# Feed-forward block products by one level of Strassen's scheme in an encoder layer on one core

## The chip, the cores and the metric

The kernel runs on one core of a Trainium2 chip. The metric is the device time of one execution in microseconds (us), lower is better. A core has five engines with instruction streams of their own, which meet only at semaphores: TensorE (PE in the profile), VectorE (DVE), ScalarE (ACT), GpSimd (POOL) and SyncE (SP), which here only issues DMAs. SBUF is the core's working memory of 128 partitions, PSUM holds TensorE's sums in eight banks of 128 x 512 float32.

## The reference

A layer of a streaming encoder over 2048 tokens (and 16 leading meta tokens) of width 1024: an input projection, two attention branches, a gated mix, a residual with layer norm, then a gated feed-forward of inner width 2816 with another residual and layer norm. All in float32. The change is in the last two lines:

```python
mix = (g_a * y_a + g_b * y_b) @ w_out
h = layer_norm(DEEPNORM_ALPHA * h + mix, ln1_g, ln1_b)
ff = (jax.nn.silu(h @ w_ff_gate) * (h @ w_ff_up)) @ w_ff_down
return layer_norm(DEEPNORM_ALPHA * h + ff, ln2_g, ln2_b)
```

## The kernel before

The program has three parts, one after the other: projection and key selection, attention (from 1129 us of the span), and `mix_and_ffn` (from 2080 us), which holds all of the mix and the feed-forward. Each part begins with SP raising every one of its semaphores by one (`begin`), since a wait is made against a value of at least one.

**Precision.** A float32 operand is kept as two rounded tiles: `hi`, a copy that ACT rounds, and `lo`, the operand less `hi`, formed by POOL for weights and by DVE for most of the rest. A product is three matmuls (`matmul3`, lines 100 to 104): hi by lo, hi by hi and lo by hi, all into one PSUM bank. Each is 128 x 128 weights by 128 x 512 columns and has a weight load of its own, which runs beside the matmul before it.

**The mix.** Tokens go in four groups of 512 (`NG`, `GROUP`), each of four tiles of 128 (`TPG`). For each group TensorE does eight `mix` blocks (two output projections, their products gated on DVE) and then `project_out`: eight chunks of `w_out`, 24 matmuls each. Weight chunks of 1024 columns per partition alternate between two raw buffers, `raw[0]` and `raw[1]`: SP loads one when POOL has used the last (`chunk`, line 2119, waits for `lo_ready`), ACT rounds it when TensorE has finished the chunk two back (`high_part`, 2201), POOL makes its low part (`low_part`, 2167). DVE adds the residual (`add1`, 2391), which frees the PSUM pairs, and normalizes (`normalize`, 2397): statistics, a reciprocal root that POOL makes (`inverse_root`), and two operations of 1024 columns. TensorE turns the result (`turn`), in the next group's mix, and ACT stores it to memory; the group that the feed-forward takes first is split at once (`high_h1`, `low_h1`).

**The feed-forward.** Four groups again. Per group TensorE runs 22 chunks of `features` (gate and up, 24 matmuls each) and then 22 row chunks of `w_down` (`natural`, 24 matmuls each), with the same two weight buffers. The feature tile is silu(gate) times up: ACT, then DVE, then ACT and DVE for its two halves (`gate`, 2297, `feature_of`, 2447), and stays in SBUF. All weights are loaded again for each group. The normalizations of a group run on DVE behind the first features of the next; the last group's have nothing behind them.

SP's order of loads, and the order on every engine, is written out by hand in these loops.

## Time and profile before

| | us |
|---|---|
| timed runs | 3996.70, 3999.55, 4012.11 (median 3999.55) |
| span of the profiled execution | 4003.8 |
| mix and feed-forward in that span | 2080 to 4003.8 |
| feed-forward's matmuls | 2507.2 to 3979.7 |

The page gives the span of the profiled execution (first to last instruction) and no other time for it. In the views below a row is a group of instructions or one instruction: when it starts, how long it took, its engine and line, the tile it writes and those it reads, and in brackets how long its engine was idle before it and what ended that. PE is busy for the modelled length of a matmul, which overlaps the next one, so the distance between starts tells its pace.

### The profile page before, as it was taken

To read this page: it belongs to the slowest core of one execution; us is meant where nothing else is said; L and a number is where in the kernel's file an instruction comes from. 1 tells how busy PE (TensorE), PEld (TensorE's weight loads), DVE (VectorE), ACT (ScalarE), POOL (GpSimd) and SP (SyncE) were. 2 spreads that over 40 slices of the span, in tenths; PEclk is the share of its full clock that TensorE was granted. 3 is DMA by queue.
4 is the path that set the end of the run, shared out by engine and by line. 5 is a ranking of instruction groups with operands and counts; after the bars stand their busy time and mean duration, and the time that the engine had idled before them with its cause. 6 is when DMAs were issued, how large, how long until landed. Compare 5 with 4: busy or idle time off the path is not lost. (4 is left out here: it accounts for less than half of the span.)

```text
span 4003.8 us, 53503 instructions
## 1 busy us (share of the span) xinstructions
PE 3708.5 (93%) x18658; PEld 3081.5 (77%) x18658; DVE 1626.6 (41%) x2432; ACT 1771.6 (44%) x3161; POOL 1612.1 (40%) x1743
## 2 busy tenths in 40 slices
PE   5998788899989999999979998999999999999997
PEld 4876566677867888989967777788878878887886
DVE  4206666886522566575425665310311031103102
ACT  3213677788425898886542222222222222222221
POOL 5213566664311322221015555444444444444443
PEclk9988899899969999999989999999999999999998
DMA  6324222422221111000025554333333423343332
GB/s 233 143 68 108 76 79 82 152 81 81 82 71 44 46 30 42 26 25 14 16 86 178 199 196 131 117 96 108 106 110 99 137 86 118 94 138 115 94 96 83
DMA packets 420920, 388.65 MB, mean 97 GB/s; under 512 B 20328, under 2 KB 361528, under 8 KB 417624
## 3 DMA queue, kind: packets, MB, share of 16 engines
q1 hardware_dynamic: 409472, 338.70, 27.8%
q10 hardware_dynamic: 11232, 47.19, 3.2%
q8 instruction: 121, 1.98, 0.2%
q14 instruction: 95, 0.78, 0.1%
HBM read 298.63 MB, written 87.20 MB: 96 GB/s over the span
## 5 line engine op out<-in xcount | busy, mean ns | idle before, releaser
L2169 POOL TENSOR_TENSOR ff_w_lo<-ff_raw,ff_w_hi 128x1024 fp32r<-128x1024 f32 x328 | 786.4, 2398 | 952.6 <-ACT ff_w_hi L2204 952.6
L2204 ACT ACTIVATE ff_w_hi<-ff_raw 128x1024 fp32r<-128x1024 f32 x328 | 346.0, 1056 | 845.7 <-PE ff_bank L104 728.8
L102 PE MATMUL ff_bank<-ff_h_hi,ff_w_lo 128*128 128x512 f32 x1408 | 551.9, 392 | 16.4 <-POOL ff_w_lo L2169 13.9
L104 PE MATMUL ff_bank<-ff_h_lo,ff_w_hi 128*128 128x512 f32 x1408 | 550.1, 391 | 0.0
L103 PE MATMUL ff_bank<-ff_h_hi,ff_w_hi 128*128 128x512 f32 x1408 | 550.0, 391 | 0.0
L102 PE MATMUL ff_bank<-ff_w_hi,ff_f 128*128 128x512 f32 x960 | 374.0, 390 | 5.5 <-DVE ff_mixed L2451 4.3
L104 PE MATMUL ff_bank<-ff_w_lo,ff_f 128*128 128x512 f32 x960 | 373.5, 389 | 0.0
L103 PE MATMUL ff_bank<-ff_w_hi,ff_f 128*128 128x512 f32 x960 | 373.5, 389 | 0.0
L1633 PE MATMUL at_ctx<-at_p_t,at_c_nat 128*128 128x128 f32 (+1 forms) x2432 | 352.2, 286 | 7.9 <-ACT at_ctx_t L1744 7.0
L1633 PEld LDWEIGHTS at_ctx<-at_p_t,at_c_nat 128*128 128x128 f32 (+1 forms) x2432 | 307.0, 194 | 37.7 <-ACT at_ctx_t L1744 13.2
L102 PEld LDWEIGHTS ff_bank<-ff_h_hi,ff_w_lo 128*128 128x128 f32 x1408 | 265.8, 189 | 76.6 <-issue 21.5
L103 PEld LDWEIGHTS ff_bank<-ff_h_hi,ff_w_hi 128*128 128x128 f32 x1408 | 265.9, 189 | 55.0
L104 PEld LDWEIGHTS ff_bank<-ff_h_lo,ff_w_hi 128*128 128x128 f32 x1408 | 265.7, 189 | 55.3
L1738 ACT ACTIVATE at_p_t<-at_turn 128x512 f32<-128x512 f32 (+4 forms) x416 | 212.9, 543 | 206.9 <-PE at_turn L1611 173.2
L2302 ACT ACTIVATE ff_f<-ff_mixed 128x512 f32 (+1 forms) x88 | 55.6, 632 | 444.6 <-DVE ff_mixed L2451 444.6
L845 PE MATMUL se_big_i<-se_ki_hi,se_qi 128*128 128x512 f32 (+16 forms) x392 | 144.4, 370 | 93.8 <-ACT se_rel L920 93.0
L1054 DVE TENSOR_SCALAR_CACHE_REDUCE se_junk_v<-late_score,se_cand 128x400 bf16<-128x400 f32 (+4 forms) x155 | 180.3, 1163 | 124.4 <-POOL se_cand L726 97.8
L1033 DVE SCALAR_TENSOR_TENSOR late_score<-se_rel,se_w_idx,late_score 128x272 f32<-128x272 f32 (+14 forms) x217 | 194.9, 898 | 73.2 <-ACT se_rel L920 66.2
L102 PEld LDWEIGHTS ff_bank<-ff_w_hi,ff_f 128*128 128x128 f32 x960 | 180.2, 188 | 45.1 <-issue 7.9
L945 ACT ACTIVATE se_junk_s<-late_score,se_cand 128x528 bf16<-128x528 f32 (+4 forms) x155 | 180.2, 1163 | 66.6 <-POOL se_cand L703 41.6
L104 PEld LDWEIGHTS ff_bank<-ff_w_lo,ff_f 128*128 128x128 f32 x960 | 180.2, 188 | 37.5
L103 PEld LDWEIGHTS ff_bank<-ff_w_hi,ff_f 128*128 128x128 f32 x960 | 180.2, 188 | 37.3
(328 smaller groups left out, 7492.0 us busy)
## 6 DMA issues: line engine op xcount, KB each, us to landing
ff_raw<-in_w_ff_gate SPq DMA_DIRECT2D x88, 512.0 KB, 3.9
ff_raw<-in_w_ff_up SPq DMA_DIRECT2D x88, 512.0 KB, 3.9
ff_raw<-in_w_ff_down SPq DMA_DIRECT2D x88, 512.0 KB, 3.5
pj_raw<-in_w_in SPq DMA_DIRECT2D x50, 512.0 KB, 4.6
proj<-se_row SPq DMA_DIRECT2D x96, 256.0 KB, 2.2
ff_f<-proj SPq DMA_DIRECT2D x64, 256.0 KB, 3.5
ff_raw<-in_w_out SPq DMA_DIRECT2D x32, 512.0 KB, 3.5
ln_x<-in_x SPq DMA_DIRECT2D x16, 512.0 KB, 5.0
```

The costliest lines, as they stand in the source:

```text
L102: pe.matmul(out, lhs_lo, rhs_hi, start=start, stop=False)
L103: pe.matmul(out, lhs_hi, rhs_hi, start=False, stop=False)
L104: return pe.matmul(out, lhs_hi, rhs_lo, start=False, stop=stop)
L845: pe.matmul(big_i[i % 2][:, a:a + n], qi_2[t % 2][:, h, :], ki_hi[:, cols], start=True, stop=False)
L945: act.activation(junk_s[:, 0:width(t)], score_of(t), ACT.Sign, bias=one(cand, 1), accum_out=one(count, 1)).then_inc(count_ready[1], 1)
L1033: dve.scalar_tensor_tensor(out=out, in0=rel[i % RELS][:, 0:wb], scalar=w_idx[:, t, h:h + 1], in1=out, op0=ALU.mult, op1=ALU.add).then_inc( ...
L1054: dve.tensor_scalar(junk_v[:, 0:width(t)], score_of(t), one(cand, 0), None, ALU.is_ge, ALU.add, accum_out=one(count, 0)).then_inc(count_re ...
L1633: last = pe.matmul(ctx[:, 0, :], c_nat[0:rows, a:a + P], p_t[v][0:rows, m, :], start=(a == 0), stop=(a + rows == w))
L1738: act.activation(p_t[v][0:rows, 0:many, :], turn[u][0:rows, 0:many * P].rearrange("p (m q) -> p m q", m=many), ACT.Copy).then_inc(turn_fre ...
L2169: pool.tensor_tensor(w_lo[u][:, :], raw[u][:, :], f32(w_hi[u][:, :]), ALU.subtract).then_inc(lo_ready[u], 1)
L2204: act.activation(w_hi[u][:, :], raw[u][:, :], ACT.Copy).then_inc(hi_ready[u], 1)
L2302: act.activation(piece(f_hi, 2 * i + n), feature[:, :], ACT.Copy).then_inc(feat_hi, 1)
```

## The change

`mix_and_ffn` is rewritten from its tiles on; the mix keeps its work. The feed-forward goes in two passes of 1024 tokens. In each, the three matrix products are cut in 2 x 2 blocks (tokens by inner width by columns) and done as seven block products with sums of blocks before and after (Strassen's scheme in the form with few sums). `PRODUCTS` and `DOWN` name them by the weight or feature block they use, `S1` to `S4` being sums.

**Features.** 11 iterations per pass, each 14 steps: product q for gate (m = 0) and up (m = 1), 12 matmuls a step. Weight blocks of a step, 512 columns, go through a ring of four slots: ACT rounds (`high_weight`), POOL makes the low part (`low_weight`), both three steps ahead. The token side `hop`, seven pairs of split tiles, stays for a pass; it comes from memory in 14 pieces (`load_h`, `high_h`, `low_h`) through two buffers. DVE makes the sums of weights (`weight_sums`, `last_sum`), ACT takes copies of running sums out of PSUM (`snapshot`), DVE adds them up (`corner`), and silu and product give four feature tiles an iteration, which SP stores to memory (`f_kept`).

**Down.** 77 steps per pass, 12 matmuls a step. Feature quadrants of 11 tiles each are read back whole; ACT and DVE split them a tile at a time (`high_a`, `low_a`), weights go through the ring (`high_b`, `low_b`). DVE sums feature tiles during products 1 and 2 and adds finished sums to the residual (`gather`).

**Jobs.** Sums of h blocks and of `w_down` blocks are made on POOL (`combine`, four dependent operations on 512 columns) and go to memory (`comb`, `down_comb`): four in `project_out` of group 2, the other 15 in feature iterations.

**Semaphores.** SP clears the first part's before attention; the last part has 79 in place of 44.

```diff
+PRODUCTS = ["A11", "A12", "S2", "S1", "S3", "A22", "S4"]
+DOWN = ["A11", "A12", "S2", "S1", "S3", "S4", "A22"]
+CELL, NPASS, RING, LEAD, NORM_AT = 4 * GROUP, 2, 4, 3, [2, 4, 6, 8]
...
             @block.sync
             def _(sp):
+                for sem in done_with:
+                    sp.sem_clear(sem)
                 s.begin(sp)
...
                     for c in range(KT):
                         load_w_out(g, c)
+                        if g == 2 and c % 2:
+                            load_job(c // 2)
+                            if c >= 3:
+                                store_job(c // 2 - 1)
+                        if g == NG - 1 and c == 1:
+                            load_raw(0)
+                            load_raw(1)
+                        if g == NG - 1 and c == 3:
+                            load_h(0)
+                            load_h(1)
+                load_raw(2)
+                for piece in range(2, 6):
+                    load_h(piece)
...
+                def load_h(piece):
+                    p, q, e = piece // (2 * NQ), piece // 2 % NQ, piece % 2
+                    if piece >= 2:
+                        sp.wait_ge(h_lo_ready, piece - 1 + START)
...
+                store_feature(NPASS * NI - 1, 3, 3)
+                for c in range(4):
+                    sp.wait_ge(feat_stored[c], 16 * NPASS * NI + START)
+                sp.wait_ge(nat_stored, 16 * NG + START)
+                load_resid(0, 0)
+                load_resid(0, 1)
+                for d in range(D_STEPS):
+                    p, q, k = of_step(d)
+                    if d + RING < D_STEPS:
+                        load_b(d + RING)
...
+                def combine(i):
+                    t = job_m[i % 2] if i < TPG else job_f
+                    b11, b21, b12, b22 = [t[:, c, :] for c in range(4)]
+                    pool.wait_ge(job_loaded[i % 2], 32 * (i // 2 + 1) + START)
+                    pool.tensor_tensor(b11, b12, b11, ALU.subtract)
+                    pool.drain()
...
+                    pool.sem_inc(job_done, 1)
...
+                low_h(0)
+                low_h(1)
+                weight_sums(0, 0)
+                weight_sums(0, 1)
+                for piece in range(2, 6):
+                    low_h(piece)
+                add1(NG - 1)
...
+                    if it == 0 and r in (2, 4, 6, 8):
+                        low_h(4 + r)
+                        low_h(5 + r)
+                        normalize(NG - 1, resid[(NG - 1) % 2], r // 2 - 1, h1_ready)
...
+                def row_sums(p, k):
+                    for u in (A21, A22):
+                        dve.wait_ge(fq_loaded[u], 16 * (p + 1) + START)
+                    dve.tensor_tensor(f_q[SUM1][:, k, :], f_q[A21][:, k, :], f_q[A22][:, k, :], ALU.add).then_inc(s_ready, 1)
+                    dve.drain()
+                    dve.tensor_tensor(f_q[A21][:, k, :], f_q[A11][:, k, :], f_q[A21][:, k, :], ALU.subtract).then_inc(s_ready, 1)
+                    dve.drain()
+                    dve.tensor_tensor(f_q[A11][:, k, :], f_q[SUM1][:, k, :], f_q[A11][:, k, :], ALU.subtract).then_inc(s_ready, 1)
+                    dve.drain()
...
+                    for a in range(TPG):
+                        if n and k == (a if q else 0):
+                            gather(*divmod(n - 1, NQ), a)
+                    if d + LEAD < D_STEPS:
+                        low_a(d + LEAD)
+                    if q == 1:
+                        row_sums(p, k)
+                    if q == 2:
+                        last_row_sum(p, k)
...
+                def product(step):
...
+                    for k in range(4):
+                        last = matmul3(pe, dst, hi[:, k, :], lo[:, k, :], hop[q][0][:, k, :], hop[q][1][:, k, :], k == 0 and q in (0, 1, 3), k == 3, q not in (0, 1, 3))
+                    last.then_inc(product_ready, 1)
...
+                for step in range(F_STEPS):
+                    product(step)
+                    if step in LAST_TURNS:
+                        turn(NG - 1, LAST_TURNS[step])
+                for d in range(D_STEPS):
+                    down(d)
```

Where the order moves: first SP's queue in `project_out` of group 2. Before, eight loads of `w_out` chunks (`in_w_out`) stand together, and the next group's output projections (`in_w_o_a`, `in_w_o_b`) follow:

```order
L2133 DMA ff_f<-proj 128x512 x4
L2122 DMA ff_raw<-in_w_out 128x1024 x8
```

Now job loads (from the turned h, line 2232) and job stores (to `comb`, line 2239) stand between them:

```order
L2196 DMA ff_raw<-in_w_out 128x1024 x2
L2232 DMA ff_raw<-h_turned 128x2x512 x2
L2196 DMA ff_raw<-in_w_out 128x1024 x2
L2232 DMA ff_raw<-h_turned 128x2x512 x2
L2239 DMA comb<-ff_raw 128x4x512
L2196 DMA ff_raw<-in_w_out 128x1024 x2
L2232 DMA ff_raw<-h_turned 128x2x512 x2
L2239 DMA comb<-ff_raw 128x4x512
```

The load of chunk 4 has moved behind the first store, that of chunk 6 behind the second.

Second, DVE's queue between the last gated product of the mix (lines 2381 and 2679) and the feed-forward. Before, `add1` (2386) is the next thing:

```order
L2374 TENSOR_TENSOR ff_part_a<-ff_bank,ff_f 128x512
L2375 TENSOR_TENSOR ff_part_b<-ff_bank,ff_f 128x512
L2381 TENSOR_TENSOR ff_mixed<-ff_part_a,ff_part_b 128x512
L2386 SCALAR_TENSOR_TENSOR ff_resid<-ff_resid,ff_bank 128x512 x8
```

Now `add1` (2688) stands behind the low halves of six pieces of h (2710) and two sets of weight sums:

```order
L2679 TENSOR_TENSOR ff_snap<-ff_snap 128x512
L2710 TENSOR_TENSOR ff_rounded_pair<-ff_resid,ff_rounded_pair 128x1024 x2
L2721 TENSOR_TENSOR ff_sum<-ff_raw 128x512
L2723 TENSOR_TENSOR ff_raw<-ff_raw 128x4x128
L2726 TENSOR_TENSOR ff_raw<-ff_sum,ff_raw 128x4x128
L2721 TENSOR_TENSOR ff_sum<-ff_raw 128x512
L2723 TENSOR_TENSOR ff_raw<-ff_raw 128x4x128
L2726 TENSOR_TENSOR ff_raw<-ff_sum,ff_raw 128x4x128
L2710 TENSOR_TENSOR ff_rounded_pair<-ff_resid,ff_rounded_pair 128x1024 x4
L2688 SCALAR_TENSOR_TENSOR ff_resid<-ff_resid,ff_bank 128x512 x8
```

Third, SP's queue at the end of the features: quadrants (line 2271), the last features' stores (2268), residuals (2284), and behind them the weights of down steps 4 and on (2281). Nothing of this kind stood there before.

```order
L2271 DMA ff_f_q<-f_kept 128x5632
L2281 DMA ff_raw<-in_w_ff_down 128x512 x4
L2271 DMA ff_f_q<-f_kept 128x5632
L2268 DMA f_kept<-ff_resid 128x512 x2
L2271 DMA ff_f_q<-f_kept 128x5632
L2268 DMA f_kept<-ff_resid 128x512
L2284 DMA ff_resid<-h_nat 128x4096 x2
L2281 DMA ff_raw<-in_w_ff_down 128x512 x18
```

## Rows read from the trace of the kernel before

**Rows 1.** The page: span, TensorE's busy time, its clock in 40 slices
```profile
span 4003.8 us, 53503 instructions
...
PE 3708.5 (93%) x18658; PEld 3081.5 (77%) x18658; DVE 1626.6 (41%) x2432; ACT 1771.6 (44%) x3161; POOL 1612.1 (40%) x1743
...
PEclk9988899899969999999989999999999999999998
```

**Rows 2.** Windows: stretch, its length, busy us (instructions) by engine, clock, DMA, GB/s
```profile
2507.20:3979.70 1472.50, 1450.99 (x6368) 1195.62 (x6368) 253.81 (x352) 386.73 (x496) 653.84 (x279) 1.00 0.35 107
```

**Rows 3.** Lines of the page: one of the three matmul lines of each kind
```profile
L102 PE MATMUL ff_bank<-ff_h_hi,ff_w_lo 128*128 128x512 f32 x1408 | 551.9, 392 | 16.4 <-POOL ff_w_lo L2169 13.9 <-DVE ff_resid L2386 2.5
...
L102 PE MATMUL ff_bank<-ff_w_hi,ff_f 128*128 128x512 f32 x960 | 374.0, 390 | 5.5 <-DVE ff_mixed L2451 4.3 <-issue 1.0
```

**Rows 4.** Timeline of all engines, two weight chunks of the features
```profile
2697.85 2.39 POOL L2169 TENSOR_TENSOR ff_w_lo<-ff_raw,ff_w_hi 128x1024 fp32r<-128x1024 f32 x1 [1.71 <-ACT ff_w_hi L2204]
...
2703.77 0.69 DVE L2453 TENSOR_TENSOR ff_f<-ff_mixed,ff_f 128x512 f32 x1 [0.93 <-ACT ff_f L2302]
...
2708.73 2.39 POOL L2169 TENSOR_TENSOR ff_w_lo<-ff_raw,ff_w_hi 128x1024 fp32r<-128x1024 f32 x1 [1.71 <-ACT ff_w_hi L2204]
```

**Rows 5.** Waits of PE from 2500 us on: in total, times, longest
```profile
PE ff_bank L102 <- POOL ff_w_lo L2169: 13.9, 9, 3.0
PE ff_bank L102 <- DVE ff_mixed L2451: 4.3, 4, 1.1
PE ff_bank L102 <- DVE ff_resid L2386: 2.5, 4, 0.7
```

**Rows 6.** Timeline of the mix at 2352 us: ACT, DVE and POOL
```profile
2351.63 1.06 ACT L2204 ACTIVATE ff_w_hi<-ff_raw 128x1024 fp32r<-128x1024 f32 x1 [6.06 <-PE ff_bank L104]
2351.64 0.69 DVE L2374 TENSOR_TENSOR ff_part_a<-ff_bank,ff_f 128x512 f32<-128x512 f32 x1 [6.74 <-PE ff_bank L104]
2352.25 0.68 DVE L2375 TENSOR_TENSOR ff_part_b<-ff_bank,ff_f 128x512 f32<-128x512 f32 x1
2352.77 2.40 POOL L2169 TENSOR_TENSOR ff_w_lo<-ff_raw,ff_w_hi 128x1024 fp32r<-128x1024 f32 x1 [3.13 <-ACT ff_w_hi L2204]
2353.14 2.57 DVE L2381 TENSOR_TENSOR ff_mixed<-ff_part_a,ff_part_b 128x512 f32<-128x512 f32 x1 [0.21 <-issue]
...
2356.46 1.29 POOL L2173 TENSOR_TENSOR ff_f<-ff_mixed,ff_f 128x512 fp32r<-128x512 f32 x1 [1.29 <-ACT ff_f L2222]
```

**Rows 7.** Timeline of PE behind a pause in the mix
```profile
2344.46 0.77 PE L102 MATMUL ff_bank<-ff_f,ff_w_lo 128*128 128x512 f32 x1 [3.21 <-issue]
2345.03 0.63 PE L103 MATMUL ff_bank<-ff_f,ff_w_hi 128*128 128x512 f32 x1
2345.45 0.63 PE L104 MATMUL ff_bank<-ff_f,ff_w_hi 128*128 128x512 f32 x1
...
2347.16 0.47 PE L102 MATMUL ff_bank<-ff_f,ff_w_lo 128*128 128x512 f32 x1
```

**Rows 8.** DMA issues: queue, count, KB each, median us to landing
```profile
ff_raw<-in_w_ff_gate SPq DMA_DIRECT2D x88, 512.0 KB, 3.9
...
ff_raw<-in_w_out SPq DMA_DIRECT2D x32, 512.0 KB, 3.5
...
pj_h_hi<-h_kept SPq DMA_DIRECT2D x2, 2048.0 KB, 10.2
pj_h_lo<-h_kept SPq DMA_DIRECT2D x2, 2048.0 KB, 15.2
```

**Rows 9.** Timeline of DVE behind the last matmul: two normalizations begin
```profile
3981.22 1.29 DVE L2399 BATCH_NORM_STATS2 ff_stats<-ff_resid 128x6 f32<-128x512 f32 x2
...
3985.86 1.28 DVE L2399 BATCH_NORM_STATS2 ff_stats<-ff_resid 128x6 f32<-128x512 f32 x2
```

**Rows 10.** Timeline at attention's start: POOL's first instruction, SP's first DMA
```profile
1129.44 0.20 POOL L108 MEMSET at_ident<- 128x128 f32 x1 [24.53 <-POOLq L553]
...
1132.15 0.38 SPq L1338 DMA_DIRECT2D at_qb<-proj  x1
```

827 lines of the change are left out of this document (567 added, 260 removed).

## The prediction, made before the changed kernel had run

> **What bounds the kernel now.** I read the page first. [rows 1] TensorE is busy for 3708.5 us of a span of 4003.8, and its clock digit stays at 8 or 9 in the second half. The change touches that half only, so the next view was the table of windows cut at the feed-forward's first and last matmul: 1472.5 us, in which TensorE ran 6368 matmuls at a clock of 1.00, and DVE, ACT and POOL were busy for 254, 387 and 654 us [rows 2]. 32 of the matmuls are transposes; the other 6336 are four groups of 1584. By line they are 3 x 1408 for gate and up, and 3 x (960 - 256) for down, 256 of each of the second kind's lines belonging to W_out [rows 3]. Then the pace: in the timeline, two weight chunks of 24 matmuls each take from one POOL instruction at 2697.85 to its like at 2708.73, so 10.88 / 48 = 0.2267 us per matmul [rows 4]. 6336 x 0.2267 = 1436 us; 36 us of the 1472 are hand-overs. The list of TensorE's waits shows 21 us of them as waits for POOL and DVE [rows 5]; the rest is transposes and restarts. The feed-forward is bound by TensorE's instruction stream, and only fewer matmuls or fewer hand-overs can shorten it.
>
> **What the change removes.** Seven products in place of eight: 22 iterations x 14 steps x 12 = 3696 matmuls for the features, 154 steps x 12 = 1848 for down, together 5544 of the same 128x512 form. 792 go: 792 x 0.2267 = **179.5 us**. The page "TensorE: Matmul & The Clock Gate" of the Trainium skill (Back-to-back issue gap) gives about 131 ns for a sustained matmul of 512 columns; by it the 792 would be worth 104 us and the time below would be 76 us longer. The trace has the same thing at 0.2267 us, and that is what counts. The old hand-overs go too, since the four groups and their loops go: **36 us**. The last product needs one sum per token tile before the final normalizations where two stood, about **1 us**. New hand-overs are priced below.
>
> **Units.** A step of 12 matmuls is 2.72 us. ACT rounds 1024 columns in 1.06 us, POOL forms their low part in 2.40 and that of 512 columns in 1.29 [rows 6]. A DVE operation on 512 columns takes 0.69 us [rows 4]; back to back they start 0.61 apart (2351.64 and 2352.25), and 0.89 apart behind a drain (2353.14) [rows 6]. DVE and POOL get in each other's way: the sum of two SBUF tiles that started at 2353.14, while POOL ran from 2352.77 to 2355.17, took 2.57 us and ended 0.54 after POOL [rows 6]. The page "SBUF — State Buffer" of the Trainium skill (Who interferes with whom) says that the lock holds in both directions, so that POOL would wait for DVE too; this trace shows only DVE waiting, and the sums below add the two engines' times, which is the same in either direction.
>
> Weights are ready three steps ahead, 8.2 us, less about 2.7 for rounding (two of ACT, one of POOL or DVE): a lag of up to **5.4 us** on these engines costs nothing.
>
> **Start of attention and of the mixing.** SP clears 53 more semaphores before attention and raises 35 more before the mixing. 46 raises took from 1129.44 to 1132.15 [rows 10], 0.059 each; both places hold back the first load: **5 us** (0 to 7).
>
> **Combinations in group 2.** Behind every second w_out chunk POOL gets a `combine` of four dependent operations, 4 x 1.29 and drains, 5.5 us; SP's `store_job` of the job before waits for it, and the next w_out load is queued behind that store. Counted from the end E1 of chunk 1: the low part of chunk 3 is done at 3.6 (1.06 + 2.40 and a hop), combine at 9.1, the load of chunk 4 at 13.0 (3.5 to land [rows 8]), its halves at 16.6. TensorE wants it at E3 = E1 + 10.9: a stall of 5.7 us. The same walk gives 4.4 at chunk 6, 5.5 at the first chunk of group 3 and 1 behind the last job: 16.6. A restart after such a pause runs at half clock: after 3.21 us of idleness matmuls started 0.42 apart until 2347.16 [rows 7], six of them at 1.2 GHz, 1.2 us lost. **21 us** in all (10 to 28).
>
> **Start of the feed-forward.** Before, h1 of its first group was already split, and `add1` came first on DVE; TensorE's longest wait for it was 0.7 us [rows 5]. Now DVE splits pieces 2 to 5 before `add1`, and `add1` frees the banks of the first product. Let S be the end of the last w_out matmul. SP issues weight buffer 2 (1 MB) and pieces 2 and 3 at S - 7.3, when the last low part is done; that is 2 MB in all, for which I take 8 us of the 10.2 that one 2 MB load took [rows 8], so S + 1. Two splits of 1.06 + 1.2 follow; pieces 4 and 5 are loaded only when these buffers are free (3.9 us for 512 KB [rows 8]) and are done at S + 10.4; the first `add1` pair ends at S + 11.8. In the first iteration DVE then has eight splits (1.2 each) and four normalizations of 4.64 us (3985.86 - 3981.22 [rows 9]), POOL waits for each variance before it may go on with weight parts, and the four transposes wait for the normalizations: walked step by step the iteration ends at S + 62 where 38.1 would do. With 3 us at the low clock: **27 us** (15 to 40).
>
> **The 22 feature iterations.** Per iteration of 38.1 us POOL has 14 x 1.29 = 18.1 us, and 5.2 more in the 15 with a job; DVE has 18 operations, 11 of them on two SBUF tiles, some 14 us and up to 11 x 0.6 of blocking; ACT 24 x 0.6. None is full, and every product waits for work at least two steps old. I take **2 us** (0 to 22, one per iteration). At the switch of passes seven pairs of h pieces go through two buffers at about 7 us a round (3.9 load, 1.06, 1.2 and hops) against 5.44 for a pair of steps, while ACT's weight rounding stands behind them: a lag of 10 less 5.4, **6 us** (0 to 12).
>
> **From features to down.** The last two quadrants of features (2.9 MB each) are read at 12 and 5.4 us before down begins, T. Two 2 MB loads issued together landed 10.2 and 15.2 us later [rows 8], so a further MB costs 2.5 us on the queue, a quadrant 7. It ends at T + 2. Then SP waits for the last feature's store, issues 4 MB of residual, and only behind them the weights of step 4: they land at about T + 16 and are split at T + 18, wanted at T + 10.9. **8.5 us** with the clock (3 to 20).
>
> **Row sums.** In product 1 of each down pass DVE has, per step, one split and three drained sums, 0.61 + 3 x 0.89 = 3.3 us, all on two SBUF tiles, and POOL 1.29 of the same: 4.6 against 2.72. 11 x 1.85 = 20 less the lead of 5.4 is 15, two passes **30 us** (2 if POOL did not exclude DVE, 36 with the gathers in the way). Normalizations during three other products: 2 splits, 4.64 and part of POOL's share against 5.44, **5 us** (0 to 20).
>
> **Sum.** 4003.8 - 179.5 - 36 - 1 + 5 + 21 + 27 + 2 + 6 + 8.5 + 30 + 5 = 3891.8. The page gives the span alone; the median of the three timed runs, 3999.55, lies 4.3 below it, so I forecast **3888 us**, 2.8% less. With all low ends it is 3818, with all high ends about 3975.
>
> **Rivals.**
> *The leads absorb most seams.* For it: all waits of the new steps are for older work, and my walks add delays in a row. Row sums at half, the start at 15, group 2 at 10, down at 3: 3888 - 15 - 12 - 11 - 5.5 = 3845.
> *DVE with POOL becomes the pace of the features.* An iteration of 40 us in place of 38.1 adds 22 x 1.9 = 42: 3930. For it: [rows 6], DVE is in order and serves three kinds of work. Against it: 18.1 + 7.7 us of exclusive use in 38.1.
> *Slower than before.* One ring of four slots serves all 462 steps. A slot is refilled only when its product has ended, so a step cannot be shorter than a third of the chain product end, ACT, POOL. I count 3 to 5 us for it (0.6 behind a snapshot of 0.6, 1.29 behind a blocked port). From 8.2 on it sets the pace; what the change saves is gone when each step is (4004 - 3892) / 462 = 0.24 us longer, at a chain of 8.9. With a silu and two snapshots always in front, at 9.5 us, a step takes 3.17: 3888 + 462 x 0.45 = 4096.
> That the change does not do what it says is excluded by its instruction list: 5544 matmuls of the same form stand there.
>
> **Chances.** Forecast 0.62 (3860 to 3920), absorbed 0.17, DVE and POOL as the pace 0.16, ring 0.05. The range 3830 to 3945 leaves out the ring, the far ends of the two others, some 0.15. About 0.5% is what a measurement of this kernel can tell from no change, 20 us. Faster by more: 0.62 + 0.17 + 0.14 = 0.93; within: 0.03 (ends of the last two cases); slower: 0.04.
>
> **What would show it.** In the profile after: 5544 matmuls with the feed-forward's names; in the middle of the features POOL's weight parts 2.72 us apart; a TensorE wait of about 11 us where the feed-forward starts, ended by DVE's `add1`; three waits of 4 to 6 us in group 2's w_out; steps of about 4.6 us late in product 1 of down, with DVE's sums 2 us long on average; one wait of 7 us at the fourth down step, ended by a DMA. It is wrong if the steps in the middle of the features are longer than 2.8 us, or if the waits named here sum to less than 50 us or more than 150.

## The result: 0.8% faster, less than a third of what was forecast

| | kernel before | changed kernel |
|---|---|---|
| timed runs, median | 4002.28 us (3996.70 to 4012.11, 4 runs) | 3970.09 us (3964.15 to 3972.44, 4 runs) |
| ratio, 95% interval | | 0.9916 [0.9897, 0.9935] |
| span of the profiled execution | 4003.8 | 3967.5 |
| forecast | | 3888, range 3830 to 3945 |

The change is faster by more than 0.5%, as the chances said, but the time lies outside the range, 82 us above the forecast. By spans it is 3967.5 against a sum of 3891.8: 76 us to find. The rest, 6 to 7 us, is the difference between spans and medians: the sum started from a span 4.3 above the median of before, and the span after is 2.6 below its own median.

### The profile after

The head of the page of the changed kernel, for [rows 1]:

```profile
span 3967.5 us, 52570 instructions
...
PE 3585.8 (90%) x17866; PEld 2941.5 (74%) x17866; DVE 2158.3 (54%) x2890; ACT 1898.4 (48%) x3537; POOL 1747.8 (44%) x2017
```

792 matmuls fewer (18658 to 17866), so TensorE should be 180 us less busy at [rows 4]'s pitch; it is 123 less. Its busy share fell from 93% to 90% as well. So each matmul costs more, and there are more pauses.

The mixing, before and after, from the tables of windows (stretch, length, busy us and instructions of PE, PEld, DVE, ACT, POOL, then granted clock, DMA share, GB/s). Kernel before:

```profile
2094.60:2507.20 412.60, 379.01 (x1632) 307.24 (x1632) 246.59 (x238) 112.43 (x148) 213.03 (x108) 0.96 0.54 178
```

Changed kernel, cut at the seams of the new feed-forward: mixing; iteration 0; iterations 1 to 9; the switch of passes (10 and 11); the other ten; then down, by products of eleven steps:

```profile
2093.60:2541.90 448.30, 389.10 (x1631) 314.31 (x1632) 247.26 (x229) 115.17 (x153) 239.50 (x127) 0.92 0.62 201
2555.80:2609.40 53.60, 47.75 (x201) 37.47 (x202) 43.35 (x50) 24.81 (x38) 23.97 (x16) 0.92 0.45 141
2609.40:2962.20 352.80, 352.80 (x1514) 283.40 (x1513) 149.28 (x163) 125.92 (x218) 229.88 (x163) 1.00 0.43 144
2962.20:3048.60 86.40, 80.56 (x338) 63.77 (x337) 52.35 (x51) 40.92 (x62) 42.66 (x29) 0.98 0.52 169
3048.60:3440.50 391.90, 391.90 (x1681) 314.84 (x1680) 164.15 (x181) 141.11 (x243) 228.98 (x164) 1.00 0.38 131
3440.50:3488.90 48.40, 33.61 (x134) 26.61 (x134) 17.89 (x15) 12.34 (x22) 15.39 (x11) 0.82 0.58 217
3488.90:3562.70 73.80, 65.51 (x265) 49.93 (x264) 68.18 (x72) 25.37 (x44) 33.36 (x22) 0.98 0.27 79
3562.70:3655.10 92.40, 92.40 (x397) 74.39 (x396) 54.27 (x48) 38.09 (x66) 43.12 (x33) 1.00 0.47 157
3655.10:3698.00 42.90, 32.97 (x133) 25.59 (x132) 37.31 (x42) 13.61 (x24) 25.48 (x16) 0.91 0.67 235
3698.00:3736.00 38.00, 34.19 (x132) 26.89 (x133) 30.56 (x36) 11.30 (x20) 19.48 (x13) 0.92 0.52 184
3736.00:3813.40 77.40, 65.72 (x265) 49.95 (x264) 71.94 (x75) 25.26 (x44) 37.04 (x24) 0.98 0.36 112
3813.40:3905.80 92.40, 92.40 (x397) 74.39 (x396) 54.15 (x48) 38.05 (x66) 42.98 (x33) 1.00 0.33 94
3905.80:3940.20 34.40, 31.48 (x133) 24.46 (x131) 29.54 (x36) 9.22 (x16) 17.80 (x12) 1.00 0.25 85
```

This table holds most of the story. Rows whose PE column equals their length (iterations 1 to 9, the other ten, three products in each pass) have no pause at all and a clock of 1.00, and still 352.8 / 9 = 39.2 us an iteration where 168 x 0.2267 = 38.1 was forecast, and 92.4 / 3 = 30.8 us for 132 matmuls where it was 29.9: 0.2333 us a matmul. In the other rows PE is short of its length. In three of them, all in down, DVE is nearly full: 68.2 of 73.8 us, 37.3 of 42.9, 71.9 of 77.4. In product 0 of the first pass it is not (17.9 of 48.4): there a load is late.

TensorE's waits from 2500 us on, for [rows 5] (engine, line, what was waited for: total, times, longest):

```profile
PE ff_bank L105 <- DVE ff_rounded_a_ring L2756: 45.2, 23, 14.8
PE ff_bank L105 <- DVE ff_resid L2688: 13.5, 1, 13.5
PE ff_bank L105 <- POOL ff_ring L2415: 7.5, 3, 3.8
```

L2756 is `low_a`, the low part of a feature tile; L2688 is `add1`. The waits are where the prediction put them, and most are larger. By stretch, in spans:

| stretch | forecast | after | miss |
|---|---|---|---|
| semaphores and all ahead of the mixing | +5 | -1 | -6 |
| mixing and start, to the first new matmul | 412.6 + 33 | 462.2 | +16.6 |
| pitch of 5544 matmuls | 0.2267 | 0.2333 | +37 |
| iteration 0 over a steady one | 15 | 14.4 | -0.6 |
| iterations and switch of passes | 2 + 6 | 8.0 | 0 |
| product 0 of down, pass 0, over 30.8 | 8.5 | 17.6 | +9 |
| row sums (products 1 and 2 over 61.6) | 30 | 28.0 | -2 |
| normalizations inside down (products 6, 0 and 6 over 30.8) | 5 | 22.9 | +18 |
| behind the last matmul | 24.1 - 1 | 27.3 | +4 |

(12 of the 27 for the start are counted in the second line, 15 in the fourth.) These add up to 76 us, which is the 75.7 to find but for rounding.

### The profile page after: what moved, and what is told of

The parts are those of the page before. It is cut to its first block and busy times, and to the rows that moved or that the text cites. A ratio compares the mean times of both kernels' runs of the same rounds, so it can differ in the third digit from the quotient of the medians.

```text
span 3967.5 us, 52570 instructions
## 1 busy us (share of the span) xinstructions
PE 3585.8 (90%) x17866; PEld 2941.5 (74%) x17866; DVE 2158.3 (54%) x2890; ACT 1898.4 (48%) x3537; POOL 1747.8 (44%) x2017
## 5 line engine op out<-in xcount | busy, mean ns | idle before, releaser
L2415 POOL TENSOR_TENSOR ff_ring<-ff_raw,ff_ring 128x512 fp32r<-128x512 f32 x264 | 379.2, 1447 | 319.0 <-ACT ff_ring L2534 316.1
L105 PE MATMUL ff_bank<-ff_rounded_pair,ff_ring 128*128 128x512 f32 x1232 | 490.0, 398 | 23.7 <-DVE ff_resid L2688 13.5
L106 PE MATMUL ff_bank<-ff_rounded_pair,ff_ring 128*128 128x512 f32 x1232 | 488.5, 397 | 0.0
L107 PE MATMUL ff_bank<-ff_rounded_pair,ff_ring 128*128 128x512 f32 x1232 | 488.5, 397 | 0.0
L2420 POOL TENSOR_TENSOR ff_ring<-ff_raw,ff_ring 128x512 fp32r<-128x512 f32 x154 | 221.4, 1442 | 232.9 <-ACT ff_ring L2579 232.8
L105 PE MATMUL ff_bank<-ff_ring,ff_rounded_a_ring 128*128 128x512 f32 x616 | 250.8, 407 | 51.4 <-DVE ff_rounded_a_ring L2756 45.2
L105 PEld LDWEIGHTS ff_bank<-ff_rounded_pair,ff_ring 128*128 128x128 f32 x1232 | 232.3, 189 | 83.1 <-issue 17.3
L2741 DVE TENSOR_TENSOR ff_snap<-ff_bank,ff_snap 128x512 f32<-128x512 f32 x132 | 91.2, 691 | 354.2 <-ACT ff_snap L2544 283.3
L105 PE MATMUL ff_bank<-ff_rounded_pair 128*128 128x512 f32 x512 | 211.9, 414 | 73.1 <-issue 33.5
L107 PEld LDWEIGHTS ff_bank<-ff_rounded_pair,ff_ring 128*128 128x128 f32 x1232 | 232.1, 188 | 57.1
L106 PEld LDWEIGHTS ff_bank<-ff_rounded_pair,ff_ring 128*128 128x128 f32 x1232 | 232.4, 189 | 56.2
L2534 ACT ACTIVATE ff_ring<-ff_raw 128x512 fp32r<-128x512 f32 x264 | 163.4, 626 | 183.4 <-PE ff_bank L107 129.5
L2579 ACT ACTIVATE ff_ring<-ff_raw 128x512 fp32r<-128x512 f32 x154 | 97.3, 632 | 319.2 <-PE ff_bank L107 267.1
L2756 DVE TENSOR_TENSOR ff_rounded_a_ring<-ff_f_q,ff_rounded_a_ring 128x512 fp32r<-128x512 f32 x154 | 184.6, 1206 | 115.8 <-ACT ff_rounded_a_ring L2571 111.8
L106 PE MATMUL ff_bank<-ff_ring,ff_rounded_a_ring 128*128 128x512 f32 x616 | 247.5, 402 | 0.0
L107 PE MATMUL ff_bank<-ff_ring,ff_rounded_a_ring 128*128 128x512 f32 x616 | 247.2, 401 | 0.0
L2387 POOL TENSOR_TENSOR ff_rounded_pair<-ff_raw,ff_rounded_pair 128x1024 fp32r<-128x1024 f32 x64 | 156.0, 2441 | 162.7 <-ACT ff_rounded_pair L2463 162.7
```

What stands on the lines that cost most here:

```text
L105: pe.matmul(out, lhs_lo, rhs_hi, start=start, stop=False, skip_group_check=goes_on)
L106: pe.matmul(out, lhs_hi, rhs_hi, start=False, stop=False, skip_group_check=goes_on)
L107: return pe.matmul(out, lhs_hi, rhs_lo, start=False, stop=stop, skip_group_check=goes_on)
L2387: pool.tensor_tensor(w_lo[u], raw[u], f32(w_hi[u]), ALU.subtract).then_inc(lo_ready[u], 1)
L2415: pool.tensor_tensor(ring[:, step % RING, 1, :].rearrange("p (k c) -> p k c", c=P), f_operand(it, q, m), f32(ring[:, step % RING, 0, :]).r ...
L2420: pool.tensor_tensor(ring[:, d % RING, 1, :], b_raw[:, d % RING, :], f32(ring[:, d % RING, 0, :]), ALU.subtract).then_inc(b_lo_ready, 1)
```

## Experiments

Each run was timed beside the kernel before on the same chip. As the medians of the kernel before moved between 3997 and 4002, ratios are what is compared; 0.001 is 4 us.

| kernel | median | ratio to before, 95% interval |
|---|---|---|
| changed kernel | 3970.09 | 0.9916 [0.9897, 0.9935] |
| `pad_pairs` | 3959.36 | 0.9896 [0.9876, 0.9916] |
| `pad_ring` | 3970.48 | 0.9929 [0.9910, 0.9948] |
| `before_pad` | 4046.20 | 1.0119 [1.0100, 1.0137] |
| `group2_order` | 3949.95 | 0.9875 [0.9857, 0.9894] |
| `pad_224` | 3936.98 | 0.9838 [0.9821, 0.9855] |
| `start_switch` | 3954.04 | 0.9877 [0.9859, 0.9896] |
| `sums_norms` | 3930.13 | 0.9821 [0.9804, 0.9839] |
| `before_half` | 3992.85 | 0.9980 [0.9970, 0.9991] |
| `start_loads3` | 3936.29 | 0.9831 [0.9811, 0.9850] |
| `all_moves3` | 3897.93 | 0.9738 [0.9722, 0.9754] |
| `all_start3` | 3893.04 | 0.9730 [0.9715, 0.9745] |
| `no_extras3` (work left out) | 3886.15 | 0.9705 [0.9688, 0.9723] |

### Why a matmul takes 0.2333 us

The steady stretches have no wait to explain it. What differs from the feed-forward before is where the operands lie. Tiles take their places in the order of declaration, and sizes in multiples of 32 bytes shift what follows. The byte addresses, per partition and modulo 512, are: kernel before, weights, h1 and features all 160; changed kernel, ring of weights (`ring`) 160, rounded h (`pair0` and on) and ring of features (`a_ring`) 448. The mixing of the changed kernel takes both operands from the `pair` tiles and runs at 0.2267.

```diff
+        pad = s.sb("pad", [P, 8])
         with Scope(nc, "ff_rounded") as r:
```

> The changed kernel with 32 bytes more in front of the tiles that hold the rounded h and the ring of rounded features; nothing else is touched. In the changed kernel the feed-forward's matmuls have their stationary operand and their moving operand 32 bytes apart modulo 64, and a step of 12 takes 2.80 us (0.2333 each); wherever both start at the same place modulo 64 (the feed-forward before, the mixing in both kernels) the pitch is 0.2267. Theory A (relative placement): the pitch goes back to 0.2267, a features iteration from 39.2 to 38.1 us, steady blocks of eleven down steps from 30.8 to 29.9, and the time falls by 5544 x 0.0067 = 37 us, to about 3933. Rival B (traffic of the other engines and the DMAs slows the matmuls): nothing changes, 3970. Rival C (the ring's slot is rewritten while its neighbour is read, or the fetch of unrolled instructions): nothing changes, 3970.

The control puts the same line ahead of `ring`:

> The changed kernel with the same 32 bytes placed in front of the ring, so that every tile behind it moves by 32 bytes too: the absolute places change, the distance between stationary and moving operand does not. Theory A in its relative form: no change, 3970 (within 5 us), iteration 39.2. If the absolute place of one of the two operands modulo 64 were the cause (stationary wanted at 0, or moving at 32), the pitch would go to 0.2267 and the time to 3933. Rivals B and C: no change.

And in the kernel before, the line stands ahead of `h1_hi`:

> The kernel before, with 32 bytes more in front of the tiles of h1 and of the features, so that these stand 32 bytes apart from the weights modulo 64, in the mixing and in the feed-forward. Theory A: 7872 matmuls (1536 of the mixing, 6336 of the feed-forward) get slower by 0.0067 us, up to 0.0078 where the features are stationary: 53 to 58 us, 4002 becomes 4055 to 4060, a pair of weight chunks takes 11.2 us instead of 10.88. Rivals B and C: the kernel before has neither the ring nor the new traffic, so nothing changes, 4002.

`before_pad` slowed by 49 us (4046.2 against 3997.0), close to the 53 expected, and with no ring and no new traffic in it: rivals B and C are out. `pad_ring` changed nothing beyond the intervals (0.9929 against 0.9916), and its pitch stayed at 0.2333. `pad_pairs`, however, gave only part: iterations of 38.45 us and blocks of down still at 30.8. So theory A was right in kind, and 64 was the wrong modulus.

```diff
-        pad = s.sb("pad", [P, 8])
+        pad = s.sb("pad", [P, 56])
```

> The changed kernel with 224 bytes in front of the tiles of the rounded h and of the ring of rounded features. The run with 32 bytes gave 0.2289 in the features (place difference 320 modulo 512) and left down at 0.2333; in every stretch that runs at 0.2267 (the feed-forward before, the mixing) the two operands stand at the same place modulo 512. Theory A2 (the difference has to be 0 modulo a power of two above 64): with 224 bytes the ring of weights, the rounded h and the ring of features all stand at 160 modulo 512; pitch 0.2267 in features and down, iteration 38.1 us, steady blocks of eleven down steps 29.9, 3970 becomes 3930 to 3936. Rival: the placement explains the features only, and down is slow because of its stationary operand from a ring that is rewritten: features at 0.2267, down still at 0.2333, 3945.

Windows of 200 us in the features and 88 us in steady down, PE alone (the x counts matmuls). Changed kernel:

```profile
2700.00:2900.00 200.00, 200.00 (x859) 1.00 0.41 134
3816.00:3904.00 88.00, 88.00 (x379) 1.00 0.33 94
```

`pad_pairs`:

```profile
2700.00:2900.00 200.00, 200.00 (x875) 1.00 0.43 140
3808.00:3896.00 88.00, 88.00 (x379) 1.00 0.33 95
```

`pad_224`:

```profile
2700.00:2900.00 200.00, 200.00 (x884) 1.00 0.40 132
3784.00:3872.00 88.00, 88.00 (x390) 1.00 0.33 98
```

859 and 379 became 884 and 390: iterations of 38.08 us and blocks of 29.92, 22 x 1.12 + 14 x 0.88 = 37 us of matmuls, of which the time shows 31 (0.9838 against 0.9916); stretches where DVE is late did not shorten. The paddings of two later runs complete the picture, read from the same windows. `start_switch` (96 bytes):

```profile
2700.00:2900.00 200.00, 200.00 (x862) 1.00 0.42 138
3809.00:3897.00 88.00, 88.00 (x380) 1.00 0.33 95
```

`sums_norms` (480 bytes):

```profile
2700.00:2900.00 200.00, 200.00 (x884) 1.00 0.41 136
3780.00:3868.00 88.00, 88.00 (x390) 1.00 0.33 98
```

| moving minus stationary, bytes modulo 512 | us a matmul | where |
|---|---|---|
| 0 | 0.2267 | before, mixing, `pad_224` |
| 256 | 0.2267 | `sums_norms`, features and down |
| 384 and 128 | 0.232 to 0.233 | `start_switch`, features and down |
| 288 and 224 | 0.2333 | changed kernel, features and down |
| 320 and 192 | 0.2289 and 0.2333 | `pad_pairs`, features and down |
| 32 and 480 | 0.2333 | `before_pad`, weights stationary and moving; the projections of the kernel before have one of the two |

In these runs the full pace of 128x512 matmuls in this form is reached where both operands stand at the same place modulo 256, and costs 1 to 3% more elsewhere. The Trainium skill's "SBUF — State Buffer" (Operand start alignment) lets an fp32 operand start at any multiple of 4 bytes and says that this is about legality, not speed; the runs here give the speed. Why the hardware does this, no run shows.

The projections of both kernels hold the same fault: h at 384, weights at 416. In the kernel before, nine matmuls take from 1117.82 to 1119.92, 0.2333 each:

```profile
1117.82 0.40 PE L103 MATMUL se_acc<-pj_h_hi,se_w_hi 128*128 128x512 f32 x1
...
1119.92 0.40 PE L103 MATMUL se_acc<-pj_h_hi,se_w_hi 128*128 128x512 f32 x1
```

```diff
+        half = s.sb("half", [P, 2])
...
         ident = s.sb("ident", [P, P])
-        half = s.sb("half", [P, 2])
```

> The kernel before with the declaration of one small tile (32 bytes) of the projection moved in front of the four h tiles, which moves these by 32 bytes and nothing else in that part: h and the weights then stand at the same place modulo 512, where they were 32 bytes apart. Theory A2: the projections' 3072 matmuls of 512 columns fall from 0.2333 to 0.2267 us, 20 us: 4002 becomes about 3982. Rival: in this part the search on the other engines, not TensorE, sets the end, and nothing changes although the pitch does; or the pitch of this part has another cause and stays.

0.9980: 8 us, not 20. PE in the first projections and in the rest up to attention, kernel before:

```profile
52.50:261.00 208.50, 208.50 (x962) 0.97 0.38 138
263.20:1126.20 863.00, 753.40 (x3194) 0.94 0.32 92
```

With the tile moved:

```profile
53.00:256.00 203.00, 203.00 (x962) 0.97 0.39 142
258.20:1119.70 861.50, 746.32 (x3194) 0.94 0.32 92
```

Where PE is without a pause, 5.5 us went; in the long stretch PE's busy time fell by 7 us and the length by only 1.5, and its longest wait there, 93 us in 65 pieces, is for ACT in the search. So the rival was right for the long stretch: a faster matmul is worth something only where TensorE sets the end.

### The combinations in group 2

> The changed kernel with one change in the order of the DMA queue: in group 2 and 3 of the mixing the store of a combination is issued one w_out chunk pair later, so that a w_out load no longer waits behind a store that waits for POOL's combine, nor lands behind its 1 MB (it took 6.0 us against 3.5 without). Theory: of the pauses of 9.2, 5.3 and 8.9 us at 2391, 2410 and 2432 and those of group 3 some 12 to 18 us go, since what is left is POOL's combine alone (5.5 us behind a low part); 3970 becomes 3952 to 3958. Rival: POOL's combine is itself the cause, because the low part of the next chunk stands behind it; then the pauses stay within 2 us each and the time falls by less than 6 us.

```diff
-                        if g == NG - 1 and n == 4:
-                            store_job(TPG - 1)
+                        if g == NG - 1 and n in (3, 6):
+                            store_job(TPG - 2 + n // 6)
...
                         if g == 2 and c % 2:
+                            if c >= 5:
+                                store_job(c // 2 - 2)
                             load_job(c // 2)
-                            if c >= 3:
-                                store_job(c // 2 - 1)
```

The changed kernel at the first of the pauses (all engines but PE; in brackets the idle time ahead and what ended it):

```profile
2379.85 1.29 POOL L2408 TENSOR_TENSOR ff_raw<-ff_raw 128x512 f32<-128x512 f32 x1
2381.21 0.38 SPq L2239 DMA_DIRECT2D comb<-ff_raw  x1
2381.64 1.56 SPq L2196 DMA_DIRECT2D ff_raw<-in_w_out  x2
...
2387.61 1.06 ACT L2463 ACTIVATE ff_rounded_pair<-ff_raw 128x1024 fp32r<-128x1024 f32 x1 [14.42 <-DMA ff_raw<-in_w_out]
```

The last operation of `combine` ends at 2381.1, SP sends the store of 1 MB and the load behind it, and the load takes 6.0 us to land (2381.64 to 2387.6). The prediction had walked exactly this queue, with 3.5 us for the load [rows 8], the median of 32 loads of the kernel before, where no such store stood in front: 2.5 us too little at this pause. The longer pauses also brought more time at 1.2 GHz: the mean granted clock of the mixing fell from 0.96 to 0.92. With the store moved, the mixing takes

```profile
2094.60:2523.30 428.70, 380.96 (x1632) 308.00 (x1632) 244.92 (x229) 115.10 (x152) 239.44 (x127) 0.96 0.65 210
```

428.7 instead of 448.3, clock 0.96: 20 us less in the profile and 16 by the ratios (0.9875 against 0.9916), within the 12 to 18 expected. The distances of 9.2, 5.3 and 8.9 us became 2.0, 2.1 and 3.7. SP's order was the larger part. What makes up the 16 us that the mixing still takes over that of before, no run separates.

### Start of the feed-forward, and the start of down

> The changed kernel with two moves and another padding. At the start of the feed-forward DVE does add1 of the last group before it splits h pieces 2 to 5; at the start of down SP issues the weights of down steps 4 to 6 before it waits for the last feature's store and before the first 2 MB of residual, and the other 2 MB eleven steps later. The padding is 96 bytes: ring and rounded h then differ by a multiple of 128 bytes but not of 256 or 512. Theory: the pause of 13.9 us in front of the first product becomes 2 to 5, part of it coming back as waits for the splits behind (net -6 to -10); the pause of 15.2 at the fourth down step and its 17 us at the low clock go but for 2 (net -12 to -17). If the placement counts modulo 128, the pitch is 0.2267 and 37 us more go: 3906 to 3915; if modulo 256 or 512, the pitch stays between 0.2289 and 0.2345 and the time is 3943 to 3952 (down to 3928 with 0.2289 in the features). Rival to the first move: pieces 4 and 5 are the limit, since they load only behind the splits of 2 and 3, and the pause moves to the third product: no gain. Rival to the second: POOL, not the load, is late at step 4, and the pause stays over 8.

```diff
-                for piece in range(2, 6):
-                    low_h(piece)
                 add1(NG - 1)
+                for piece in range(2, 6):
+                    low_h(piece)
...
-                store_feature(NPASS * NI - 1, 3, 3)
...
-                load_resid(0, 0)
-                load_resid(0, 1)
                 for d in range(D_STEPS):
...
+                    if d == 2:
+                        store_feature(NPASS * NI - 1, 3, 3)
...
+                        load_resid(0, 0)
+                    if d == NI:
+                        load_resid(0, 1)
```

Iteration 0 and product 0 of down in this kernel:

```profile
2550.20:2614.00 63.80, 50.55 (x201) 39.90 (x202) 48.82 (x54) 26.98 (x40) 23.66 (x16) 0.84 0.45 144
3442.10:3481.30 39.20, 33.66 (x133) 26.49 (x132) 18.19 (x15) 12.11 (x22) 16.18 (x11) 0.91 0.69 250
```

The second move worked in part: 48.4 us became 39.2, 9 us of the 12 to 17 expected, and TensorE still waits 5.5 us there, for DVE's low parts. What stood on SP's queue ahead of step 4's weights was the cause, as predicted; only the wait was 14.8 and not 7. The edit moved the wait for the last store and the 4 MB of residual together, so it does not say what each of them cost. The first move gave nothing. The pause in front of the first product shrank from 13.9 to 4.2 us, and iteration 0 grew from 53.6 to 63.8: the rival.

> The changed kernel with 224 bytes of padding and two more edits. (1) Start of the feed-forward: h pieces 2 and 3 are loaded ahead of the third raw weight buffer, the first pieces are rounded one w_out chunk earlier, and DVE's order is pieces 0 and 1, first weight sums, pieces 2 and 3, add1, second weight sums, pieces 4 and 5. (2) The normalizations in down stand at steps 1, 4, 6, 8. Against 3937 for the padding alone. Theory: the run that only put add1 first moved the pause behind the third product, since pieces 4 and 5 load only when 2 and 3 are split; with both early the pause of 13.7 us in front of the first product becomes 2 to 5 and none comes back, -9; the last normalization no longer stands in front of the gathers of product 6, so the 10.9 us pause at the pass switch of down becomes 3 to 5, and the normalizations cost 14 in place of 25, -11: 3914 to 3920. Rival: DVE has a fixed load of splits, add1 and normalizations there, and what is gained in front of the first product is lost in iteration 0 (53.1 us becomes 60 or more): only the 11 us, 3926.

```diff
-                load_raw(2)
-                for piece in range(2, 6):
-                    load_h(piece)
+                load_h(2)
+                load_h(3)
+                load_raw(2)
+                load_h(4)
+                load_h(5)
...
+                low_h(2)
+                low_h(3)
+                add1(NG - 1)
+                weight_sums(0, 1)
+                low_h(4)
+                low_h(5)
```

Neither edit paid: 0.9831 against 0.9838 for the padding alone, and 3936 us is above the rival's 3926 too. The pause fell to 2.0 us and iteration 0 took 60.2 (13.7 and 53.1 with the padding alone), so that 4.6 us of the two were won and the rest only moved, as the rival said. In down, products 6, 0 and 6 with the normalizations took 111.2 us in place of 115.3, but products 1 and 2 of the two passes took 156.0 in place of 150.7, and down as a whole 495.4 against 494.7: the 11 us that theory and rival both counted on did not come. TensorE's longest waits in iteration 0 are now

```profile
PE ff_bank L105 <- POOL ff_ring L2418: 10.5, 3, 5.6
```

L2418 is POOL's low part of the ring's weights: POOL stands in its own order behind the variances of `normalize`, which DVE reaches late. The delay is mostly the sum of DVE's splits, `add1` and normalizations; their order chooses where TensorE pays, and little more.

### Row sums and normalizations in down

> The changed kernel with DVE's work in down spread out: in pass 0 the first two sums of quadrant blocks 0 to 7 are formed in product 0 (steps 3 to 10) in place of product 1, and the normalizations stand three steps apart (1, 4, 7, 10) in place of two. The padding is 480 bytes: operands 256 bytes apart modulo 512. Theory: a round of one normalization and two splits takes DVE 8.1 us where two steps last 5.6, so each normalization adds 2.5 of lag; at three steps a round is 9.2 against 8.4 and the lead of 5 us absorbs it: the 22 us of products 6, 0 and 6 fall to 3 to 7. Row sums of pass 0: 12 us fall to 0 to 3, those of pass 1 (16 us) stay. In all -24 to -31: 3939 to 3946 at a pitch of 0.2333, and some 37 less (3902 to 3909) if 256 bytes apart is as good as the same place. Rival: it is not DVE's order but its share of the port with POOL that is full in product 0 too, so that the sums make product 0 late by what product 1 gains: -15 at most.

```diff
-CELL, NPASS, RING, LEAD, NORM_AT = 4 * GROUP, 2, 4, 3, [2, 4, 6, 8]
+CELL, NPASS, RING, LEAD, NORM_AT = 4 * GROUP, 2, 4, 3, [1, 4, 7, 10]
...
+                    if q == 0 and (p, k) in EARLY:
+                        first_sums(p, EARLY[p, k])
                     if q == 1:
                         row_sums(p, k)
```

Products 1 and 2 of pass 0 took 64.8 us where `pad_224`, at the same pitch, took 72.8: the row sums gave 8 of the 9 to 12 expected. The products with normalizations took 6.9 us less, of 15 to 19 expected, with a pause of 10.9 us at 3665, since the last normalization now stood in front of the gathers; steps 1, 4, 6, 8 (`start_loads3`) brought that pause to 8.0, and the products to 4 us under `pad_224`. So down was 15 us shorter, not 24 or more; the time, 3930, is 21 above the theory's 3902 to 3909, and 6 of these lie in the mixing and ahead of it, where nothing was edited and the profiled execution was later than that of `pad_224` (first new matmul at 2559.3 against 2553.6). DVE in the changed kernel, one round:

```profile
3671.79 1.29 DVE L2694 BATCH_NORM_STATS2 ff_stats<-ff_resid 128x6 f32<-128x512 f32 x2
...
3675.22 2.31 DVE L2703 SCALAR_TENSOR_TENSOR ff_resid<-ff_resid,ff_rstd,ff_ln 128x1024 f32<-128x1024 f32 x1 [0.44 <-POOL ff_rstd L2395]
3677.63 2.18 DVE L2756 TENSOR_TENSOR ff_rounded_a_ring<-ff_f_q,ff_rounded_a_ring 128x512 fp32r<-128x512 f32 x2
3679.90 1.28 DVE L2694 BATCH_NORM_STATS2 ff_stats<-ff_resid 128x6 f32<-128x512 f32 x2
```

8.1 us from round to round (3671.79 to 3679.90) for two steps of TensorE, 5.6. The normalization alone is 5.7, not the 4.64 of [rows 9]: its last operation takes 2.31 here beside POOL. To tell DVE's added work from everything else, one kernel leaves it out:

> Leaves out all row sums of down (the products read the unsummed quadrants) and the body of the twelve normalizations that lie inside down; with 224 bytes of padding. It prices what DVE adds in down. Theory: in the padded kernel the blocks of eleven steps last 49.2, 38.0, 34.9, 29.9 x3, 42.7 in pass 0 and 38.5, 41.0, 36.9, 29.9 x3, 33.8 in pass 1, 56 us over 14 x 29.92 without the 19 of the transition; sums 31, normalizations 25. All blocks but the first fall to 29.9 to 31, the time from 3937 to 3881 to 3886. Rival: part of these waits belongs to the gathers into the residual and to POOL's half of the rounding, which stay: blocks of 32 to 34 remain where banks are handed over, 3895 to 3905.

```diff
+                    if NG <= stage < NG + 2 * NPASS - 1:
...
+                        return
...
-                    dve.tensor_tensor(f_q[SUM1][:, k, :], f_q[A21][:, k, :], f_q[A22][:, k, :], ALU.add).then_inc(s_ready, 1)
...
+                    dve.sem_inc(s_ready, 3)
```

Its windows for products 1 and 2, product 6 of pass 0, products 0 and 1 with 2 of pass 1, and the last:

```profile
3472.00:3531.80 59.80, 59.80 (x266) 49.51 (x265) 35.41 (x31) 25.39 (x44) 28.39 (x22) 1.00 0.34 97
3621.60:3652.50 30.90, 30.05 (x134) 24.59 (x132) 19.04 (x22) 13.46 (x24) 16.43 (x16) 1.00 0.80 271
3652.50:3682.70 30.20, 30.20 (x132) 24.61 (x133) 18.29 (x18) 11.70 (x21) 17.23 (x15) 1.00 0.84 306
3682.70:3742.60 59.90, 59.90 (x266) 49.58 (x265) 36.10 (x31) 25.37 (x44) 28.60 (x23) 1.00 0.44 136
3832.30:3862.30 30.00, 30.00 (x133) 24.59 (x131) 15.60 (x20) 9.22 (x16) 12.52 (x12) 1.00 0.33 114
```

Every one is full, PE's busy time equal to its length or within a microsecond. 0.9705 against 0.9838 is 53 us, the 51 to 56 expected. The gathers, the ring and POOL's rounding, all still there, cost nothing by themselves; row sums and normalizations together cost all of it. How the sum divides, 28 and 23 us in the changed kernel, is read from the products in which each stands and was not run apart. DVE and POOL do slow each other: in the changed kernel's product 1 POOL's weight part takes 1.50 us on average where it takes 1.29 here:

```profile
L2420 POOL TENSOR_TENSOR ff_ring<-ff_raw,ff_ring 128x512 fp32r<-128x512 f32 x12 | 18.0, 1497 | 22.8 <-ACT ff_ring L2579 22.8
```

That is the other direction of [rows 6]. The prediction said that the trace of before shows only DVE waiting; it shows POOL late too. Its 512 columns, 1.29 us in [rows 6], took 2.28 beside an operation of DVE:

```profile
2327.24 1.70 DVE L2404 SCALAR_TENSOR_TENSOR ff_resid<-ff_resid,ff_mv,ff_ln 128x1024 f32<-128x1024 f32 x1
2327.81 2.28 POOL L2173 TENSOR_TENSOR ff_f<-ff_mixed,ff_f 128x512 fp32r<-128x512 f32 x1
```

Both traces agree with the Trainium skill's "SBUF — State Buffer" (Who interferes with whom), which states the lock for both engines.

### The edits together

> All edits that paid, in one kernel: 224 bytes of padding (-33), the store of combinations one pair of chunks later (-21), the weights of down steps 4 to 6 ahead of the residual (-9), the first row sums of pass 0 in product 0 (-9), normalizations at steps 1, 4, 6, 8 (-11), and the small tile of the projection moved (-7). Theory: they lie in different stretches and add: 3970 - 90 = 3880, 3.0% below the kernel before. Rival: work that comes earlier collides with something else that was hidden by the pauses (combine with the mixing, row sums behind a shorter transition), and a third of the seams' gain is lost: 3895.

> The same kernel with the edits at the start of the feed-forward too (pieces 2 and 3 earlier, add1 between them and 4 and 5). Theory: another -9, 3871. Rival: no difference to the kernel without them (3880), because in iteration 0 DVE's splits and normalizations set the pace.

Both beat both kernels. `all_start3` is at 0.9730 [0.9715, 0.9745] of the kernel before, 2.7%, where the change as made has 0.8%. They fall 18 to 22 us short of the theories; `all_moves3` is at its rival. Stretch by stretch against the changed kernel: the mixing starts 2.8 us earlier (7 booked for the small tile), mixing and start take 21.9 less (21 booked), the features 21.4 less (24.6 by pitch; the switch of passes took 87.2 us in place of 86.4), and down 25.5 less, where pitch, weights ahead of the residual, sums and normalizations were booked at 41. In down the edits do not add: products 6, 0, 1 and 2 between the passes took 41.7 + 36.8 + 78.2 = 156.7 us, and 159.0 in `pad_224`, though the normalizations alone had been booked at 11. DVE is the pace there, so neither the faster matmuls nor another order shortens them by much. The step from 0.9738 to 0.9730 by the start's edits is inside the intervals: 13.9 + 52.7 us became 2.0 + 59.7, 5 us by the profile.

## Why the prediction was wrong

- **What the change removes.** 792 matmuls at 0.2267 went, and 36 us of old hand-overs. Right in count. The step that failed is the silent one behind it: that the 5544 that stay "of the same 128x512 form" keep the pitch of [rows 4]. They took 0.2333, 37 us, half of the miss; `pad_224` gave it back in the matmuls and 31 us in the time, 3937, which lies inside the range. Shape, type and count were the same, and the operands' places were not. The projection's matmuls, in the trace of before, would have shown it: the same form, without a pause, at another pitch.
- **Semaphores.** At attention's start TensorE's pause, in which SP clears them, grew from 8.9 to 12.4 us (3.1 had been worked out from [rows 10]); ahead of the mixing it grew by 0.5. The rest of the -6 is the profiled execution: attention was 7 us shorter and the projection 2.5 longer, with no other edit in either.
- **Combinations in group 2.** The walk was right, its load time was not: 3.5 us is the landing of a load alone, and behind a 1 MB store on the same queue it was 6.0. The mixing took 35.7 us more where 21 were forecast, +14.7 with the clock, and 16 to 20 could be had back by SP's order (`group2_order`).
- **Start of the feed-forward.** 27 predicted; 13.9 in front and 14.4 in iteration 0, as worked out. Two experiments tried other orders: one won nothing, the other 4.6 us in the profile and nothing clear in the time.
- **Iterations and switch.** 2 + 6 predicted, 8.0 measured. No iteration in the steady part has a pause; the rival in which DVE and POOL become the pace there is out, and so is the ring.
- **From features to down.** Mechanism right, size off by a factor of two: 7 us of pause became 14.8, and the row of product 0 has a mean clock of 0.82, 17 of its 48.4 us at 1.2 GHz. The walk had the last feature's store land at once; SP waited 7 us for it, while a 2.9 MB quadrant was on the same queue:

```profile
3443.39 0.32 SPq L2268 DMA_DIRECT2D f_kept<-ff_resid  x1
3450.62 0.79 SPq L2284 DMA_DIRECT2D ff_resid<-h_nat  x2
```

- **Row sums.** 30 predicted, 28 measured, with luck in it. The round of one split and three sums was taken as 4.6 us; it lasts 3.93:

```profile
3526.63 0.69 DVE L2756 TENSOR_TENSOR ff_rounded_a_ring<-ff_f_q,ff_rounded_a_ring 128x512 fp32r<-128x512 f32 x1
...
3530.56 0.69 DVE L2756 TENSOR_TENSOR ff_rounded_a_ring<-ff_f_q,ff_rounded_a_ring 128x512 fp32r<-128x512 f32 x1
```

  All 30 were put in product 1 of the two passes. Product 1 had 18 of the 28, and product 2, which has the last of the sums and had no term of its own, the other 10.
- **Normalizations in down.** 5 predicted, 22.9 measured: the worst ratio. The step took 4.64 us for one from a place where POOL has nothing else to do [rows 9]. 8.1 us against 5.6, four times in a row, is a lag of 10 against a lead of 5.4, and the gathers of the product's end come on top, with the lead already spent, so that the next product starts late too. `no_extras3` shows that without sums and normalizations nothing of it is left.
- **Tail.** DVE still had a normalization in hand at the last matmul (3940.2), gathered from 3942.2 and began the final normalizations at 3945.3, 5.1 us behind it, where it was 1.5 in [rows 9] (3979.7 to 3981.2): +3 where -1 was forecast.
- **The rivals.** The leads did not absorb the seams, they were spent; the ring was never the pace; DVE with POOL became the pace, but in down between the passes and not in the features, where it had been looked for.
- **The range** left out what hung on the one number that was never given a bound. All priced terms had two ends; the pitch, which was multiplied by 5544, had one. The ends were also added up wrongly: with the shift of 4.3 they give 3813 and 3968, not 3818 and 3975, so that the measured 3970 lies even above the sum of all high ends.
- **The signs.** They would not have raised an alarm by themselves: the steps in the middle lasted 2.80 us, just at the limit of 2.8, and the waits named sum to some 80 us, between 50 and 150.

## What to carry to other kernels

A pitch measured for one pair of tiles is not a property of the instruction's shape: before it is multiplied by thousands, compare it over all stretches without pauses in the trace, and try a stationary and a moving operand at the same place modulo 256 bytes (a pad of 56 words was worth 0.8% here, as much as the whole rewrite). Another engine's added work in a window is first priced as its total against TensorE's time in that window, at durations measured beside the other engine; leads are used up once. Even that total is a lower bound: in product 6 of the first pass DVE had 37.3 us of work against 30.8 us of matmuls, and the product took 42.9. And a load's landing time is read for what stands in front of it on its queue.

## What was unexpected in the hardware

The dependence on placement: 0.2267 us at a distance of 0 or 256 bytes modulo 512, 0.2289 to 0.2333 at the others that were run, with the clock at 1.00 and no pause. Distances of 64 and 96 bytes were not run, nor was it tried which of the two reads is the slow one.
